# One-tile first group: a hybrid trunk step split into five token groups instead of four, with keys and values of attention loaded in different turns

## What is computed

```python
mod = silu(c) @ w_mod + b_mod                      # conditioning: shift, scale, gate (twice)
h = modulate(x, norm1_gain, sh1, sc1)
z = h @ w_in                                       # gq gk gv gr glr | dq dk dv | gates
o_a, gla_state = gla_recurrence(q, k, v, log_a, h0)      # carried over all earlier tokens
y_a = (rmsnorm(o_a) * silu(gr)) @ w_gla_out
p = softmax(q1 k1^T) - lam * softmax(q2 k2^T)      # prompt: causal by chunks of 64 keys;
o_b = p @ v                                        # sample: 512 cached keys + 32 new ones
y_b = rmsnorm(o_b) @ w_diff_out
x = x + gt1 * ((sigmoid(g_a) * y_a + sigmoid(g_b) * y_b) @ w_out)

h2 = modulate(x, norm2_gain, sh2, sc2)
q = (h2 @ w_pq)                                    # 8 retrieval heads
v1, i1 = top_k(q[..., 0] @ sub_keys1.T, 16); v2, i2 = top_k(q[..., 1] @ sub_keys2.T, 16)
sc, ci = top_k(v1[:, None] + v2[None, :], 16); idx = e1 * 128 + e2; g = softmax(sc)
ff = sum_k g_k * gelu(h2 . peer_u[idx_k]) * peer_v[idx_k]     # 8 x 16 = 128 experts per token
y = x + gt2 * ff
```

## Time and profile before

| | us |
|---|---|
| median of 3 executions | 4738.47 |
| lowest, highest | 4728.97, 4742.68 |
| span of the profiled execution | 4756.0 |

### The profile page before, as it was taken

One profiled execution on the slowest core, in us unless ns is written; L12 is line 12 of the kernel. 1 busy time (PEld: TensorE's weight loads), 2 busy tenths in 40 slices (PEclk: granted clock), 3 DMA queues, 4 the chain that ended last, 5 costly groups with the idle time before them and its releaser, 6 DMA issues. The chain is left out here.

```text
span 4756.0 us, 46362 instructions
## 1 busy us (share of the span) xinstructions
PE 3136.8 (66%) x14944; PEld 1913.5 (40%) x14944; DVE 2683.4 (56%) x7493; ACT 1308.3 (28%) x2813; POOL 1228.0 (26%) x1067
## 2 busy tenths in 40 slices
PE   6887846886797258876975397884569743333333
PEld 4675744553564035543753064552247420000000
DVE  2133145578544765788344755676542476675675
ACT  2344102446301034556010225544530200000000
POOL 0000002233223232323122322222211224454453
PEclk8886977787898568887987597787789865555555
DMA  7422439898999898889999897776678979999998
GB/s 266 140 80 84 176 109 345 343 378 304 347 385 382 326 376 341 350 322 357 363 379 374 310 325 263 294 260 232 243 269 299 348 265 379 409 415 397 397 405 333
DMA packets 274250, 1470.61 MB, mean 309 GB/s; under 512 B 46920, under 2 KB 89000, under 8 KB 107960
## 3 DMA queue, kind: packets, MB, share of 16 engines
q0 software_dynamic: 152064, 1107.36, 59.5%
q1 hardware_dynamic: 121944, 360.27, 21.2%
HBM read 1426.39 MB, written 40.01 MB: 308 GB/s over the span
## 5 line engine op out<-in xcount | busy, mean ns | idle before, releaser
L1635 POOL DMA_INDIRECT rt_ring<-in_peer_uv,rt_few_idx x1056 | 1224.7, 1160 | 3497.1 <-PE rt_acc L809 2592.7
L1582 DVE SCALAR_TENSOR_TENSOR rt_ring<-rt_ring,rt_h 128x1024 f32<-128x1024 f32 x1056 | 1262.6, 1220 | 399.7 <-DMA rt_ring<-in_peer_uv,rt_few_idx 372.0
L809 PE MATMUL rt_acc<-rt_ring,rt_diag 128*32 128x512 f32 x4224 | 810.7, 846 | 956.5 <-DVE rt_diag L1593 952.6
L809 PEld LDWEIGHTS rt_acc<-rt_ring,rt_diag 128*32 128x32 f32 x4224 | 101.5, 126 | 1412.2 <-DVE rt_diag L1593 1252.2
L558 PE MATMUL pair<-w,dense 128*128 128x256 f32 (+1 forms) x2288 | 549.4, 399 | 28.6 <-DMA w<-in_weights 17.2
L569 PE MATMUL pair<-dense,w 128*128 128x256 f32 (+1 forms) x2336 | 548.9, 393 | 4.9 <-DMA w<-in_weights 4.4
L1144 ACT ACTIVATE rt_act_dot<-rt_dot 128x2 f32<-128x2 f32 x528 | 106.3, 202 | 1557.1 <-DVE rt_ring L1582 1544.8
L558 PEld LDWEIGHTS pair<-w,dense 128*128 128x128 f32 (+1 forms) x2288 | 431.3, 192 | 173.9 <-issue 71.5
L569 PEld LDWEIGHTS pair<-dense,w 128*128 128x128 f32 x2336 | 444.0, 192 | 124.2 <-issue 43.5
L1593 DVE TENSOR_SCALAR rt_diag<-cst,rt_act_dot,rt_few_prob 128x32 f32<-128x32 f32 x1056 | 266.5, 297 | 189.3 <-ACT rt_act_dot L1144 177.4
L558 PE MATMUL bank<-w,dense 128*128 128x256 f32 (+1 forms) x1168 | 282.3, 399 | 28.5 <-DMA w<-in_weights 13.2
(11 more groups left out here) (236 smaller groups left out, 3062.3 us busy)
## 6 DMA issues: line engine op xcount, KB each, us to landing
w<-in_weights SPq DMA_DIRECT2D x232, 1024.0 KB
rt_ring<-in_peer_uv,rt_few_idx POOLq DMA_INDIRECT x1056
rt_h<-scratch_h SPq DMA_DIRECT2D x132, 128.0 KB
dense<-scratch_mod SPq DMA_DIRECT2D x18, 512.0 KB, 13.7
dense<-in_x_prompt SPq DMA_DIRECT2D x16, 512.0 KB
scratch_scores<-dense SPq DMA_DIRECT2D x64, 128.0 KB
rt_sc<-scratch_scores SPq DMA_DIRECT2D x8, 1024.0 KB
rt_x<-scratch_x SPq DMA_DIRECT2D x132, 32.0 KB
```

The source lines that it names most:

```text
L809: mm = nc.tensor.matmul(acc[u % 2][a * T:(a + 1) * T, :], diag[b % 2][:, i, :], slot[:, D + c * BANK:D + (c + 1) * BANK], start=(q == 0), ...
L1582: dt = nc.vector.scalar_tensor_tensor(up, up, 1.0, h2[u % 2][:], ALU.mult, ALU.mult, accum_out=dot[:, b % 2, i:i + 1])
L1635: nc.gpsimd.indirect_dma_start(ring[n % RING][:], None, d["peer_uv"], bass.IndirectOffsetOnAxis(ap=few_idx[u % 2][:, c:c + 1], axis=0)).th ...
```

## The change

It does two things. `GROUPS` becomes (0), (1, 2), (3, 4), (5, 6), (7, 8), so that the widths are 128, 256, 256, 256 and 160 columns and the fill holds tile 0 alone. All sizes that come from `GROUPS` follow, among them the rows of ticks and the number of batches beside them: the stages of group 1 now stand beside 54 of the 64 batches of tile 0's four units.

A buffer for attention now holds the keys of load m and the values of load m - lag. A load is one head of the group's last prompt tile, or of the sample tile. The lag is 3 where each tile of the group has loads of its own (groups 0 and 4), otherwise 1 (two tiles share a head's load). The buffer is given back at the later of the last scores from its keys and the last product with its values (`kv_done`). Group 0 and group 4 so have 11 and 19 buffer turns, the others 9.

```diff
-GROUPS = ((0, 1), (2, 3), (4, 5), (6, 7, 8))
+GROUPS = ((0,), (1, 2), (3, 4), (5, 6), (7, 8))
+def kv_loads(g):
+    kinds = [t for t in GROUPS[g] if t == NT or t == max(i for i in GROUPS[g] if i < NT)]
+    return [(h, t) for h in range(DH) for t in kinds]
+def kv_lag(g):
+    return 3 if len(kv_loads(g)) == DH * len(GROUPS[g]) else 1
+def kv_load_of(g, x):
+    nt = len(GROUPS[g])
+    per = len(kv_loads(g)) // DH
+    return x // nt * per + (1 if GROUPS[g][x % nt] == NT else 0)
...
-    for h in range(DH):
-        names += [("kv", h)] + ([("kvs", h)] if GROUPS[g][-1] == NT else [])
+    names += [("kv", m) for m in range(len(kv_loads(g)) + kv_lag(g))]
...
+def kv_parts(g, m):
+    loads = kv_loads(g)
+    return [(part, *loads[i]) for part, i in (("k", m), ("v", m - kv_lag(g))) if 0 <= i < len(loads)]
...
+        kv_done = []
+        for g in range(NG):
+            last = {}
+            for k, row in enumerate(ATTEND[g][1]):
+                if row["score"] is not None:
+                    last[kv_load_of(g, row["score"])] = k
+                if row["apply"] is not None:
+                    m = kv_load_of(g, row["apply"][0]) + kv_lag(g)
+                    last[m] = max(k, last.get(m, k))
+            kv_done.append({k: [m for m in sorted(last) if last[m] == k] for k in set(last.values())})
...
-                    wt = weights((g, "kv" if t < NT else "kvs", h))
+                    slot = (g, "kv", kv_load_of(g, x))
+                    wt = weights(slot)
...
+                    released[slot] = (at_scored[1], base + x + 1)
...
-                    v = W[WPOS[g, "kv" if t < NT else "kvs", h] % NW][:, D:].rearrange("p (t c) -> p t c", c=VD)
+                    slot = (g, "kv", kv_load_of(g, x) + kv_lag(g))
+                    v = weights(slot)[:, D:].rearrange("p (t c) -> p t c", c=VD)
...
-                    released[g, "kv" if t < NT else "kvs", h] = (at_applied, G + 1)
+                    released[slot] = (at_applied, G + 1)
```

More of the change, by code:

```diff
@@ L105, with transfers @@
 HPOS = {n: i for i, n in enumerate(HOST)}
+def kv_parts(g, m):
+    loads = kv_loads(g)
+    return [(part, *loads[i]) for part, i in (("k", m), ("v", m - kv_lag(g))) if 0 <= i < len(loads)]
+def transfers(name):
+    if name[1] != "kv":
+        return 1
+    return sum(2 if t == NT else 1 for part, h, t in kv_parts(name[0], name[2]))
 def load_count(j):
-    return sum(2 if WEIGHTS[i][1] == "kv" else 4 if WEIGHTS[i][1] == "kvs" else 1 for i in range(j % NW, j + 1, NW))
+    return sum(transfers(WEIGHTS[i]) for i in range(j % NW, j + 1, NW))
 def ticks(g):
@@ L846, in finished @@
             if kind == "at":
[L847 to L855, removed]
+                return [(a[0], "kv", m) for m in kv_done[a[0]].get(a[1], ())]
             if kind == "merge":
@@ L1646, in load_weights @@
                 if name[0] == "kv":
-                    h, last = name[1], max(t for t in GROUPS[g] if t < NT)
-                    nk = (last + 1) * P
                     stored(g)
[L1650 to L1657, removed]
+                    for part_, h, t in kv_parts(g, name[1]):
+                        nk = (t + 1) * P
+                        if part_ == "k" and t < NT:
+                            sp.dma_start(dst[:, 0:nk], d["kT"][h, :, 0:nk]).then_inc(at_, 16)
+                        elif part_ == "v" and t < NT:
+                            sp.dma_start(dst[:, D:D + nk], d["vh"][h, :, 0:nk]).then_inc(at_, 16)
+                        elif part_ == "k":
+                            sp.dma_start(dst[:, 0:PAST], d["cache_kT"][h]).then_inc(at_, 16)
+                            sp.dma_start(dst[:, PAST:PAST + DEC], d["kT"][h, :, SEQ:SEQ + DEC]).then_inc(at_, 16)
+                        else:
+                            sp.dma_start(dst[:, D:D + PAST], d["cache_vh"][h]).then_inc(at_, 16)
+                            sp.dma_start(dst[0:DEC, D + PAST:D + PAST + VD], d["vh"][h, 0:DEC, NT * VD:(NT + 1) * VD]).then_inc(at_, 16)
                 else:
@@ L1685, in _ @@
             sp.dma_start(wa[:], d["w_alpha"][0]).then_inc(const_in, 16)
-            load_x(0)
-            load_x(1)
+            for t in GROUPS[0][:2]:
+                load_x(t)
             sp.wait_ge(filled, FILLS)
```

## The result

The changed kernel takes 4664.0 us (median of 4 executions, 4661.5 to 4669.0) against 4740.6 (4, 4729.0 to 4747.6) for the kernel before. The ratio is 0.9844 with a 95% interval of 0.9823 to 0.9865, which is 77 us less. The forecast was 4711.5 in a range of 4625 to 4795: right in direction, but with 27 us of gain only, a third of what was measured. The profiled execution has a span of 4659.7 us, against 4729 in the forecast.

What follows compares the result with a forecast made beforehand. No engine bounds the whole: DMA bounds the tail, PE and chains the fill. Stretches 500 + 784 + 982 + 1010 + 1000 + 453 = 4729, 27 less than 4756; on the timed median 4711.5, range 4625 to 4795.

Steps and rivals of the forecast that it cites:

- the price of the further phase: Across the gather phases: a fourth phase, paid for against savings at both ends, costs 536 us.
- the dense stages of phase 0: Tile 1 and 2 work beside the first tile's gathers, up to the end of keys: 656 us (638 to 673).
- The fill: Stretch before any gather, now one tile: halved columns halve PE's pass time, 500 us against 722.
- The rival of the lost clock: Before the first gather: thin tiles run weight passes at the low clock, +60 us, 4771 in all; chance 0.12.
- The tail: Gathers alone at the end, five units for nine: 341 us less at 394 GB/s, 453 us.
- the price of a batch: Beside dense work in the first gather phase: each of 49 gather batches lengthens the stages by 1.4 us.
- The first rival: First gather phase: dense work is bound by its own chains and loads and doesn't speed up; +128 us, 4839; chance 0.18.
- Phases 1 and 2: Middle gather phases, eight units and two tiles each: 982 us (965 to 990) and 1010 us (1000 to 1030).
- Phase 3: Gathers beside tiles 7 and 8: cheaper merge, keys and attention, dearer GLA and loads; 1000 us (960 to 1030).
- The rival that the rule would cost 50 us: Attention in the last three gather phases: products wait for values that come a turn later; +50 us, 4761; chance 0.10.
- The gain rival: Attention and first gather phase gain more: cheaper batches, no store waits, shorter later phases; 4631 in all; chance 0.20.
- the sign: Whole kernel: a small difference of large terms, hanging on the one-tile start and dense work beside half the batches; faster 0.48.

## Why the forecast was right, and where it was not

The direction was right, and the gain was put at 27 us where 77 were measured. The step that failed is the price of the further phase, 536 us for a measured 484. In it three terms were too high: the dense stages of phase 0 (656 for 625), the base of phase 2 (999.6 for 987.5), and the last group's phase (1000 for 975.6).

**The fill: right** (500, measured 496.6). Halving the columns halves the passes, as forecast: merge and keys came out at 61.6 and 35.4 for 61 and 35. That the sum is right to 3 us is in part luck: dk and dv took 95.2 for 88, where the clock had indeed gone from 0.88 to 0.79, and mix and shift 31.8 for 27, and GLA at 96.1 for 105 and attention at 41.3 for 50 made up for them. The rival of the lost clock is refuted at its size: the granted clock is 0.79 in dk, dv and GLA, between the levels of 1.2 and 2.4 GHz (0.50 and 1.00), and the fill is 63 us under the 560 of that rival. In dk and dv the 16 passes behind a wait of 3.0 to 4.2 us for a load took 5.2 to 6.3 us, between the 3.5 of full speed and the 6.7 of the low level, as one such burst (5.41) did before. The rule of the Trainium skill ("TensorE: Matmul & The Clock Gate", HAM oscillation) speaks of tiles whose compute is shorter than the wait for the next load. The trace agrees in part, in these slow bursts. But a round here computes some 7 us for a wait of 3, so that I applied the rule beyond its case when I priced the rival by it; and the 0.50 of attention was there with two tiles too.

**The tail: right** (453, measured 450.4), since it is bytes over a measured rate.

**Phase 0: the term that failed is the price of a batch.** The forecast put the dense stages at 656 us: 573 + 14 of base and 49 batches at 1.4. The runs give 625: a base of 574, 47 batches at 0.83, which is 39, and 12 in the mix. So the base was 13 too high and the batches 18 (69 for 51). The size of each share hangs on the 0.83, which rests on two profiled executions; the sum does not. I had taken 1.4 from between the 1.05 of the merge and the 1.76 of all of group 1's stages. The upper end was read from stages on a full DMA with waits for loads in them, and outside the mix the price is even under the lower end. With half the batches DMA is busy for 0.65 to 0.80, and I read the low price as batches that fill gaps in which PE waits for other engines anyway; no run shows that by itself. The stretch behind was 120.8 for 110, as 14 batches (112 records) stood there for the 10.5 forecast, at 4.8 each and not 3.8. The first rival, a dense row that does not speed up, needed more than 683 and is refuted.

**Phases 1 and 2: the step that failed is the base.** I took the 999.6 of one profiled execution for phase 1, and the second has 987.5 (988.9 with the rule and the old groups). With that base the +10 for 128 more keys gives 997.5, for 992.8 measured. Phase 1 at 982 is right, though not by its reason: the rule gives nothing to groups of wide pairs, and the mean of the two phases in the second profile is 984 by itself. The same base is why the timed forecast is off by 47.5 only, while the spans are off by 69. The 17.5 us by which that execution was longer than the timed ones were taken off again at the end, and the changed kernel's median is 4.3 over its span, not under it.

**Phase 3: 24 too high, by terms that partly cancel.** Stage by stage against phase 1 of the first profile, the base of the forecast, the merge saved 31 us (103.3 for 134.2) where 22 were forecast, and GLA cost 12 more (221 for 209) where it was put at 30. Keys saved 8 for 5, and attention cost 12 more (203.6 for 191.1) where it was to save 3. Mix and shift cost 14 more, and dk and dv, dq and the stretch behind saved 23 together, which the forecast had left unchanged. The merge's row:

```profile
3808.50:3911.80 103.30, 90.25 (x625) 75.15 (x625) 40.36 (x96) 6.98 (x30) 23.07 (x24) 0.95 1.01 421
```

I had set a floor by the tail's 394 GB/s, and DMA moved 421 here. The attention is dearer because 34.0 us of waits for exp take the place of the waits for keys, as they did in group 3 with the old groups; my 10.0 a pair, the old time less its waits for loads, has no room for the wait that comes next, and a pair took 12.7.

**What the forecast didn't ask** is what each half of the change is worth. It took the 107 us of waits out of the last group's attention only within the price of phase 3, and so put down to the groups what is the rule's: the old groups with the rule give all of the gain, and the new groups with lag 1 at the end give 0.9977. With the rule in both kernels the further phase costs 571 us for 567 saved; it came out at 484 only because the old phases still held 87 us that the rule removes. The rival that the rule would cost 50 us, with waits for values, is refuted; no wait of PE for values is among the longest. The gain rival's 4631 was nearest by mechanism: the waits for loads and the cheaper batches that it named are what was found. It had added 80 us of gain to the forecast, and 47.5 of them came on the timed median; its phase 1 at 967 did not come at all (980.3).

**As to the sign**: forecast 0.48 for faster by over 0.3%, and it is faster by 1.6%. The groups alone, which were the large terms, did come out near zero, as 222 + 341 against a further phase suggested. What moved the time was a term that I had kept at a few us in phases 0 to 2, and inside a stage's price in the last one.

## What to carry to other kernels

When a rotating buffer holds two things that are given back at different times, let it hold parts of different loads. Here it was worth 84 us of 4743 with the old groups, and in the last of the new ones the lag decides over 69 us. When a change has two parts, price each with the other undone before adding large terms of opposite sign. Work that can run beside a stage or behind it should be priced in both places: here some 1 us beside, 4 to 5 behind as long as more than a dozen are left there. Moving four batches in each phase gave 66 us, where the regrouping gave nothing that can be measured. A price read from two runs wants a third: here one stage moved by 12 us with the order and hid it. And take the base of a stretch from two profiled executions where a dozen us matter.

## What the runs showed of the hardware

- DMA moved 421 GB/s over the 103 us of the last merge, with weights and gathers in flight, and 394 at most over a tail of gathers alone. The Trainium skill ("DMA: Bandwidth & Descriptors", Specifications) lists about 358 GB/s for a core's share of HBM; with one core at work the trace goes beyond it in both.
- A batch's matmuls keep PE busy for 1.24 us (64.11 us for 51.5 batches), and outside the mix a batch lengthens the dense stages of phase 0 by 0.6 to 0.8 us, with PE busy for 0.9 of them.
- Sixteen weight passes of 256 columns behind a wait of 3 to 4 us for a load took 5.2 to 6.3 us, where full speed gives 3.5.
- Taking away 112 us of waits for loads gave 74; 31 came back as waits for the next engine in the chain, ACT's exp.
